# A feed-forward block's instruction stream on TensorE: unrolled, or a loop of five iterations

## The reference, cut to what matters

```python
def swiglu(x, w_gate, w_up, w_down):
    return (jax.nn.silu(x @ w_gate) * (x @ w_up)) @ w_down

h = h + rmsnorm(swiglu(rmsnorm(h, norm_g[i, 2]), w_gate[i], w_up[i], w_down[i]), norm_g[i, 3])
h = h + jax.nn.sigmoid(h @ w_ple_gate[i]) * (p[i] @ w_ple[i])
```

## Time and profile before

| what | value |
|---|---|
| runs | 3248.37, 3249.73, 3247.97 us; median 3248.37 |
| profiled execution | 3248.37 us, its span 3246.7 us |
| TensorE matmul busy | 3131.3 us, 96% of the span |
| vector, scalar, GpSimd busy | 48%, 28%, 8% |
| mean granted TensorE clock | 0.992 |
| TensorE matmuls | 20,580, each with a weight load |

### The profile page before, as it was taken

How to read it: one execution, slowest core, us unless ns; L and a number is a source line. 1 busy time by engine, 2 the same in 40 slices (tenths; PEclk the granted TensorE clock), 3 DMA queues, 4 the chain that set the end, 5 groups by cost and what they waited for, 6 DMA issues and landing times.

```text
span 3246.7 us, 52192 instructions
## 1 busy us (share of the span) xinstructions
PE 3131.3 (96%) x20580; PEld 2978.5 (92%) x20580; DVE 1564.0 (48%) x2681; ACT 907.3 (28%) x1640; POOL 266.6 (8%) x319
## 2 busy tenths in 40 slices
PE   7999999999999999999999998989999999999999
PEld 6999989999999998999987776549899999999989
DVE  5444365444444446543335555443654444444462
ACT  3111242111111116422225554333421111111252
POOL 1000010000000001000015551110100000000011
PEclk9999999999999999999999999999999999999999
DMA  2111111111111111113227765971011111111112
GB/s 90 45 39 45 47 33 46 46 46 42 44 46 46 46 60 33 46 46 115 69 61 149 146 118 194 337 291 53 26 51 41 46 46 46 46 45 40 60 46 68
DMA packets 234053, 238.88 MB, mean 74 GB/s; under 512 B 18806, under 2 KB 191862, under 8 KB 233859
## 3 DMA queue, kind: packets, MB, share of 16 engines
q1 hardware_dynamic: 209842, 156.26, 16.6%
q0 software_dynamic: 24016, 79.77, 8.3%
HBM read 201.11 MB, written 18.10 MB: 68 GB/s over the span
## 4 chain that ended last, share of the span: by engine, by line
PE 89%; DVE 5%; ACT 3%; issue 2%; DMA 1%; POOL 1%; DVEq 0%; ACTq 0%; POOLq 0%
PE psum L2040 20%; PE psum L2042 20%; PE psum L2041 20%; PE psum L2066 5%; PE psum L2060 5%; PE psum L2061 4%; PE psum L2525 2%; PE psum L2570 2%; PE psum L2509 2%; PE psum L2494 1%; PE psum L2589 1%; PE psum L2619 1%; PE psum L2495 1%; DVE xs_lo L1529 1%; DVE xs_lo L1743 1%
## 5 line engine op out<-in xcount | busy, mean ns | idle before, releaser
L2040 PE MATMUL psum<-xs_hi,w_hi 128*128 128x384 f32 (+1 forms) x2784 | 911.1, 327 | 0.3
L2042 PE MATMUL psum<-xs_hi,w_lo 128*128 128x384 f32 (+1 forms) x2784 | 908.0, 326 | 0.0
L2041 PE MATMUL psum<-xs_lo,w_hi 128*128 128x384 f32 (+1 forms) x2784 | 907.4, 326 | 0.0
L2040 PEld LDWEIGHTS psum<-xs_hi,w_hi 128*128 128x128 f32 x2784 | 522.7, 188 | 0.9 <-DVE w_lo L1309 0.8
L2041 PEld LDWEIGHTS psum<-xs_lo,w_hi 128*128 128x128 f32 x2784 | 522.7, 188 | 0.0
L2042 PEld LDWEIGHTS psum<-xs_hi,w_lo 128*128 128x128 f32 x2784 | 522.5, 188 | 0.0
L778 ACT ACTIVATE w_hi<-raw 128x1024 fp32r<-128x1024 f32 x192 | 202.2, 1053 | 536.4 <-DVEq L1325 526.1
L1659 DVE TENSOR_TENSOR y<-y,psum 128x384 f32<-128x384 f32 x528 | 269.1, 530 | 168.7 <-PE psum L2042 168.7
L2042 PE MATMUL psum<-hid_hi,w_lo 128*128 128x384 f32 (+1 forms) x1056 | 346.0, 328 | 0.0
L2040 PE MATMUL psum<-hid_hi,w_hi 128*128 128x384 f32 (+1 forms) x1056 | 345.6, 327 | 0.0
L2041 PE MATMUL psum<-hid_lo,w_hi 128*128 128x384 f32 (+1 forms) x1056 | 345.1, 327 | 0.0
(11 more groups left out here) (300 smaller groups left out, 3894.4 us busy)
## 6 DMA issues: line engine op xcount, KB each, us to landing
kpage<-in_cache_k SPq DMA_DIRECT2D x64, 512.0 KB, 7.2
v_page<-in_cache_v POOLq DMA_DIRECT2D x64, 512.0 KB, 5.5
raw<-in_w_gate SPq DMA_DIRECT2D x44, 512.0 KB, 3.7
raw<-in_w_up SPq DMA_DIRECT2D x44, 512.0 KB, 3.6
raw<-in_w_down SPq DMA_DIRECT2D x44, 512.0 KB, 3.7
raw<-in_w_in SPq DMA_DIRECT2D x24, 512.0 KB, 3.6
raw<-in_w_ple_gate SPq DMA_DIRECT2D x16, 512.0 KB, 3.6
k_hh<-kT_scratch POOLq DMA_DIRECT2D x32, 256.0 KB, 6.4
```

Source lines behind the costliest of these rows:

```text
L2040: M(out, wh, xh, start=first, stop=False)
L2041: M(out, wh, xl, start=False, stop=False)
L2042: return M(out, wl, xh, start=False, stop=last)
```

## The change

TensorE's ten steps become a hardware loop of five iterations of two steps, `pe.Fori(0, 5)`. `gate_up` and `down` get the iteration i and hand it to `slab`, and the block numbers that go into the accumulator waits and the chunk numbers that go into the `hid_ready` wait are now expressions of i. The first gate_up and the last down stay outside. Other engines, tiles, loads and the arithmetic are the same.

```diff
-                def gate_up(n, blk, first=False):
+                def gate_up(n, blk, i=None, first=False):
                     if first:
                         first_pair(layer)
                     for u in range(2 if first else 0, 4):
-                        slab(n + u)
+                        slab(n + u, i, 12)
                         block8(blk + u, u, n + u, xs_hi, xs_lo, None, pre_rows if first else None,
                                u - 2 if first else None)
...
-                def down(n, blk, chunks, par, last=False):
+                def down(n, blk, chunks, par, i=None, last=False):
 
                     pe.wait_ge(hid_ready, chunks * NT + NT)
                     for s in range(2):
-                        slab(n + s)
+                        slab(n + s, i, 12)
...
-                gate_up(n0, b0, True)
-                for g in range(10):
-                    gate_up(n0 + 6 * g + 4, b0 + 12 * g + 4)
-                    down(n0 + 6 * g + 8, b0 + 12 * g + 8, c0 + 2 * g + 2, g % 2)
-                down(n0 + 64, b0 + 124, c0 + 22, 0, True)
+                gate_up(n0, b0, None, True)
+                with pe.Fori(0, 5) as i:
+                    gate_up(n0 + 4, i * 24 + (b0 + 4), i)
+                    down(n0 + 8, i * 24 + (b0 + 8), i * 4 + (c0 + 2), 0, i)
+                    gate_up(n0 + 10, i * 24 + (b0 + 16), i)
+                    down(n0 + 14, i * 24 + (b0 + 20), i * 4 + (c0 + 4), 1, i)
+                down(n0 + 64, b0 + 124, c0 + 22, 0, None, True)
```

## The result

The rolled kernel takes 3272.3 us (median of 4 runs, 3270.9 to 3272.9) against 3248.2 us before: ratio 1.0078, 95% interval 1.0061 to 1.0093, so 24 us slower. The forecast was 3257.2 us with a range up to 3266.

A forecast was written before the change was run, and what follows sets the result against it. TensorE's own instruction stream was taken to bound the stage; all terms cost nothing except eight branch misses of 1.1 us, so 3248.37 + 8.8 = 3257.2 us, range 3247 to 3266.

The forecast's parts named there:

- TensorE's own stream: In the rolled FFN stage only this sets the time; any stall reaching the array adds to the end one for one.
- The register waits: 86 waits per iteration depending on i, about 0.1 us each, hidden under the matmuls: cost nothing.
- the slab wait on the sequencer: lo_ready wait moves ahead by the sequencer's lead, 2.8 us; slab ready 6.8 us before its first load: cost nothing.
- the taken branches by themselves: Four per layer, eight in all, target still in instruction memory, 0.21 to 0.24 us each: cost nothing.
- The first block: Loop body's first instruction block, overwritten at each of 8 branches and fetched again: 1.1 us each, 8.8 us; chance 0.53.
- F: Time to ask for, move and take in one instruction block at a missed branch: taken as 3.3 us, less 2.2 cover.
- Two misses at a branch: Rival: loop head near a block's end, following block missing too, uncovered; 13 us more in that layer, 3270; chance 0.08.
- The memory would have to hold at least 9: Body lies in 8 or 9 blocks, fetched ahead; keeping the first needs 9 held, rows show no more than about 5.

The follow-up runs named there:

- the kernel with the hint: Changed kernel plus a branch prefetch hint as first instruction of every iteration, both layers rolled: 3248.0 us, ratio 1.0002 to the kernel before.
- the head on slot 0: Changed kernel, both layers rolled, with layer 1's loop head placed on the first instruction of a 256-instruction block: 3253.6 us, ratio 1.0019 to the kernel before.
- 239: Changed kernel with layer 1 unrolled and layer 0's loop head 17 instructions before the end of its 256-instruction block: 3269.7 us, ratio 1.0061 to the kernel before.
- slot 229: Changed kernel with layer 1 unrolled and layer 0's loop head 27 instructions before the end of its 256-instruction block: 3257.9 us, ratio 1.0028 to the kernel before.
- the shortened kernel with slot 85: Changed kernel less 32 instructions an iteration (one low-by-high product left out), loop heads on instruction 85 of a 256-instruction block, body in 8 blocks: 3232.3 us.

## Why the prediction was wrong

**Right, and shown.** TensorE's own stream sets the time of the stage: every stall of the sequencer beyond its queue came out one for one (25.5 us by parts, 25.3 between the branches, below). The register waits, the slab wait on the sequencer and the taken branches by themselves cost nothing that can be told: the kernel with the hint has all of them and stands at 1.0002 (0.9993 to 1.0011). One slab is not ready far ahead, as the prediction took all to be: the one at a loop's entry, whose load waited 0.4 us for w_lo already before. There the moved wait costs 0.1 us a layer (the load starts 0.15 us after w_lo is done in layer 1, 0.05 before). The first block is gone at each of the eight branches (3.3 to 3.8 us each, with a packet on q8 0.9 to 1.0 us in). Its price was put at 1.1 us each, 8.8 us in all; the gaps measured 8.7 us (4.2 and 4.5). F was taken as 3.3 us on top of the branch; the branches lasted 3.3 to 3.8 us, against 0.2 for a hit, so F is 3.1 to 3.6.

**The step that failed** is the price of layer 1's branches: the prediction charged each of its four with one miss, 1.1 us, and left the second miss behind it to a rival, "Two misses at a branch". The runs showed both misses at all four, 9.9 us for the second ones, and 6.9 us of half clock behind them. The rival was named, with its place (layer 1, "the head's place in the second layer shifts by what is cut from the first") and with 3270 us as its time. It was given 0.08, and the range, up to 3266, left it out. Its reason was that only the shift spoke for it. Its condition was not shown then; the heads set by hand show it, with second gaps of 8.5 us in four with 17 instructions left in the head's block and 4.2 with 27. But where the shift leads can be counted: the rows give one packet per 256 instructions, so the place of a block's end in the stream is known, and so is the length of what is cut. The count after the fact (six pairs and two register instructions before the stop) puts the head 14 instructions before the end of its block. Also unasked was how wide the bad range of places is: with 14, 17, 27 and once with 43 instructions left there is a second gap, so it is not a few slots in 256 but some forty.

**A size within it.** The second miss was put at 3.3 us without cover, 13 us for the layer; it was 9.9 us, since six pairs, at 0.17 us each, and the way into the block cover about a microsecond. And a term was missing: the clock. The prediction read the clock at 1.00 in the stage and did not ask what a standstill of some microseconds does to it. It added 6.9 us. That the rival's 3270 lies near the measured 3272.3 is in part luck: its second miss was put too high and its clock at nothing. 8.7 + 9.9 + 6.9 = 25.5 us, against 25.3 between the branches in the profile (the 6.9 is what was left of it in layer 1; the direct count gives 7.2) and 24.1 in the timed runs.

**Also off**: the reason for the eviction. "The memory would have to hold at least 9" holds only where the ninth has been asked for by the time of the branch: with the head on slot 0 three branches of layer 1 in a row found their target, 0.21 to 0.23 us, with eight held. In the change itself it always had been (in layer 0 a packet 3.0 to 5.6 us before each taken branch), and in layer 1 the body, 14 instructions in the head's block and 1,802 behind them, reaches into nine blocks by itself; with the heads elsewhere the ninth had not always been asked for.

## What to carry to other kernels

Count the blocks of a loop's body on TensorE, 256 instructions each, from where the head lies and with register instructions included. Here a body in 7 blocks had no miss at 8 branches (0.21 to 0.22 us each), and its time was 23.4 us under before for 23 us of work left out; one that ended 24 instructions into the eighth missed 2 of 8, one that ended 77 in 5 of 8, and the change 8 of 8. Past 7, use a branch hint, which kept this body whole in both layers (ratio 1.0002), or unroll. Where the queued work hides most of a stall, look at what comes right behind it with an empty queue: the second stall and the clock that fell behind it cost layer 1 nearly four times what the first did (9.9 + 6.9 us against 4.5).

## What the runs showed of the hardware that was not expected

- The same loop in one layer cost 5 to 22 us by where its first instruction lay: 3252.6 us with 43 instructions left in its block by count (layer 1), 3257.9 with 27 and 3269.7 with 17 (layer 0).
- The granted clock fell to 0.50 for 3.4 to 6.8 us after each second gap of 1.7 us and over (with 239, and in the changed kernel), and after none of those with slot 229, 0.6 to 1.7 us. The two sets touch, and the single gap of 2.1 us in the shortened kernel with slot 85 left the clock full, so the length of the gap alone is not what decides. Nor is the sum of an edge's two gaps: 2.6 us lost the clock with 239, 2.9 kept it with 229. What decides was not pursued.
- A hint for the branch kept the body whole, 100 packets on q8 against 171, in layer 1 although it reaches by count into a ninth block.
